# A linear attention with its forward decays moved into the projection, scores issued one tile early, backward keys on GpSimd, and norms taken tile by tile

## The reference, cut to what matters

```
la = log_sigmoid(l_a @ w2 + b) / 16            # per direction, 4 heads x 64
b = cumsum(la within a chunk of 64)             # the backward direction on flipped tokens
a = (q*exp(b - b_ref)) @ (k*exp(b_ref - b)).T, lower triangle
o = a @ v + (q*exp(b)) @ s_in
u = (k*exp(b_last - b)).T @ v;  s_next = exp(b_last)*s + u
y = rmsnorm_head(o_f)*g*silu(g_f) + rmsnorm_head(o_b)*g*silu(g_b)
```

## Time and profile before

| | |
|---|---|
| median of 3 runs | 1501.27 us (1497.28 to 1501.35) |
| the profiled execution | 1498.48 us, span 1496.7 us |
| busy, share of the span | PE 88%, PEld 68%, DVE 55%, ACT 46%, POOL 7% |
| chain that ended last | PE 75%, DVE 10%, DMA 7%, ACT 5% |
| mean granted TensorE clock | 0.948 of 2.4 GHz |
| projection of layer 0 ends | 213.15 us (216.72 less the wait of 3.57) |
| attention's first scores, layer 0 | 286.15 us |
| projection of layer 1 ends | 873.81 us |
| attention's first scores, layer 1 | 952.07 us |

### The profile page before, as it was taken

The page is one execution under the profiler, slowest core; times in us unless marked ns, Lnnn a source line. Parts: engine busy times, 40 slices in busy tenths (PEclk is TensorE's granted clock), DMA queues, the critical chain, the costliest instruction groups (busy, mean ns, idle before and its releaser), DMA issues.

```text
span 1496.7 us, 19449 instructions
## 1 busy us (share of the span) xinstructions
PE 1313.9 (88%) x7024; PEld 1020.9 (68%) x7024; DVE 817.0 (55%) x1174; ACT 691.3 (46%) x989; POOL 104.8 (7%) x93
## 2 busy tenths in 40 slices
PE   4799977679899999999989957795899999999993
PEld 0576655357688888888869843484688888888882
DVE  0412277773533332323343484654688988898882
ACT  2622343263532311322243452354577877787771
POOL 4000010001111100111210010020000000000001
PEclk9899998799999999999989979898899999999997
DMA  9365623201122321223212428343799999999992
GB/s 347 116 231 202 231 74 140 86 1 56 58 99 88 127 83 68 99 99 123 88 46 99 157 104 312 115 167 135 267 349 389 369 356 360 384 369 358 357 351 99
DMA packets 96383, 282.76 MB, mean 189 GB/s; under 512 B 8577, under 2 KB 10017, under 8 KB 96193
## 3 DMA queue, kind: packets, MB, share of 16 engines
q1 hardware_dynamic: 90592, 262.17, 48.1%
q0 software_dynamic: 3568, 12.19, 2.2%
q10 hardware_dynamic: 2160, 7.55, 1.4%
HBM read 271.39 MB, written 10.49 MB: 188 GB/s over the span
## 4 chain that ended last, share of the span: by engine, by line
PE 75%; DVE 10%; DMA 7%; ACT 5%; issue 3%; POOL 0%; POOLq 0%; ACTq 0%; SPq 0%; DVEq 0%
PE ps L635 12%; PE ps L636 12%; PE ps L637 12%; PE ps L1008 5%; PE ps L1010 5%; PE ps L1009 5%; DMA raw<-in_w_mod 3%; PE ps L612 3%; PE ps L1022 3%; PE ps L1024 3%; PE ps L1026 3%; DVE wlo L529 2%; DMA raw<-in_w_fm 1%; PE ps L870 1%; PE ps L707 1%
## 5 line engine op out<-in xcount | busy, mean ns | idle before, releaser
L529 DVE TENSOR_TENSOR wlo<-raw,whi 128x1024 fp32r<-128x1024 f32 (+2 forms) x271 | 349.1, 1302 | 310.8 <-ACT whi L524 309.9
L524 ACT ACTIVATE whi<-raw 128x1024 fp32r<-128x1024 f32 (+2 forms) x271 | 298.7, 1108 | 297.4 <-PE ps L637 147.9
L635 PE MATMUL ps<-hhi,whi 128*128 128x512 f32 (+1 forms) x736 | 277.6, 377 | 23.7 <-DVE hlo L1569 22.6
L636 PE MATMUL ps<-hlo,whi 128*128 128x512 f32 (+1 forms) x736 | 273.9, 372 | 0.0
L637 PE MATMUL ps<-hhi,wlo 128*128 128x512 f32 (+1 forms) x736 | 273.7, 372 | 0.0
L635 PEld LDWEIGHTS ps<-hhi,whi 128*128 128x128 f32 x736 | 139.6, 190 | 60.5 <-issue 29.6
L636 PEld LDWEIGHTS ps<-hlo,whi 128*128 128x128 f32 x736 | 139.9, 190 | 26.5
L637 PEld LDWEIGHTS ps<-hhi,wlo 128*128 128x128 f32 x736 | 139.4, 189 | 27.1
L529 DVE TENSOR_TENSOR xlo<-raw,xhi 128x1024 fp32r<-128x1024 f32 (+1 forms) x98 | 131.9, 1353 | 19.4 <-ACT xhi L524 17.2
L524 ACT ACTIVATE xhi<-raw 128x1024 fp32r<-128x1024 f32 (+1 forms) x98 | 113.3, 1165 | 44.4 <-PE ps L1026 33.3
L1008 PE MATMUL ps<-whi,hs_hi 128*128 128x512 f32 (+1 forms) x256 | 96.3, 376 | 2.5 <-DVE hs_lo L1895 2.5
(11 more groups left out here) (279 smaller groups left out, 2076.3 us busy)
## 6 DMA issues: line engine op xcount, KB each, us to landing
raw<-in_w_gu SPq DMA_DIRECT2D x230, 512.0 KB, 5.4
raw<-in_w_dn SPq DMA_DIRECT2D x80, 704.0 KB, 8.7
raw<-in_w_mod SPq DMA_DIRECT2D x96, 512.0 KB, 4.7
raw<-in_w_fm SPq DMA_DIRECT2D x32, 512.0 KB, 3.5
raw<-in_w_out SPq DMA_DIRECT2D x16, 512.0 KB, 4.8
raw<-in_w_tg SPq DMA_DIRECT2D x8, 512.0 KB, 3.5
y_rows<-back POOLq DMA_DIRECT2D x1, 4096.0 KB, 16.8
y_rows<-ys ACTq DMA_DIRECT2D x8, 512.0 KB, 4.6
```

The costliest lines, as they stand in the source:

```text
L524: nc.scalar.activation(high(v)[:, 0:cols], src[:, 0:cols], ACT.Copy).then_inc(hi_ready, 1)
L529: nc.vector.tensor_tensor(low(v)[:, 0:cols], landed_in(v)[0][:, 0:cols], high(v)[:, 0:cols].bitcast(F32), ALU.subtract).then_inc(lo_ready, 1)
L635: nc.tensor.matmul(outp, whs, xh, start=first, stop=False)
L636: nc.tensor.matmul(outp, whs, xl, start=False, stop=False)
```

## The change

- The forward logits are multiplied after SB. ACT takes their absolute value and softplus behind the split issued at SB+1, with a table load before and, after SC+1, one back; DVE does minimum, sum and scan there (`decay_sum`, `decay_scan`), the keys at SC and the reference keys at SC+1. The first gate unit on PE waits for the forward scan (`d_ready` of 1), as it writes the same banks.
- In `gla` PE issues tile m+1's scores ahead of tile m's outputs, the modulation pairs behind the outputs, and turns the backward keys at step 3 ahead of that step's outputs. ACT's and DVE's orders follow that. The backward minimum moves behind state 0, the backward scan to step 1.
- GpSimd multiplies the backward keys and reference keys (`later_keys`), behind its six memsets.
- Squares and norms are taken for all forward outputs at once (group 0) and for each backward tile apart (`squares`, `normed_heads`, `head_norms`); PE turns each tile when it is ready.

```diff
+                def logits(l, dr):
+                    for p in range(GT):
+                        nc.tensor.matmul(ps[:, 2 + 2 * dr + p, :], w2[32 * dr:32 * dr + 32, l, p * P:(p + 1) * P],
+                                         la[32 * dr:32 * dr + 32, :], start=True, stop=True).then_inc(z_done[l], 1)
...
+                        if m == SB:
+                            pe.wait_ge(v_out[l], NTT)
+                            logits(l, 0)
                         if m == AQ:
 
                             pe.wait_ge(g_out[l], len(list(gla_reads(l))))
-                            for dr in range(2):
...
+                            logits(l, 1)
...
                         if m == 0:
-                            pe.wait_ge(v_out[l], NTT)
+                            pe.wait_ge(d_ready[l], 1)
                         tm(v, m, 512, 2 if l else 0)
...
+                for n, (dr, step, t) in enumerate(todo):
+                    m = rd.index(n) if n in rd else None
+                    if m is not None and issued[0] == m and n == 0:
+                        pe.wait_ge(kt_out[l], GT)
+                        scores(m)
+                    updates(n)
+                    if n == NTT - 1:
+                        keys_turned(1)
+                    if m is not None:
+                        if issued[0] == m:
+                            scores(m)
+                        if m + 1 < len(rd) and todo[rd[m + 1]][0] == dr:
+                            scores(m + 1)
+                        outputs(m)
+                    if n == 0:
+                        pe.wait_ge(z_out, l + 1)
+                    if n == NTT - 1:
+                        pe.wait_ge(kt_out[l], 2 * GT)
+                    for k in gla_pairs(l, n):
+                        mod_pair(PAIR_GLA[l] + k)
...
-                    if kind == "fm" and f == AQ + 1:
+                    if kind == "fm" and f == SB + 1:
                         logits_abs(l, 0)
+                        nc.scalar.preload_act_table_set("natural_log_exp_and_others")
                         softplus(l, 0)
-                    if kind == "fm" and f == AQ + 2:
+                    if kind == "fm" and f == SC:
                         key_exp(l, 0)
-                    if kind == "fm" and f == AQ + 3:
+                    if kind == "fm" and f == SC + 1:
                         ref_exps(l, 0)
+                        nc.scalar.preload_act_table_set("silu_and_others")
...
+            def later_keys(l):
+
+                pool.wait_ge(zeroed[l], 3)
+                pool.wait_ge(e_ready[l], 5)
+                nc.gpsimd.tensor_tensor(gk[:, :, :], gk[:, :, :], lk[:, :, :], ALU.mult).then_inc(e_used[l], 1)
+                pool.wait_ge(at_done[l], len(gla_reads(l)))
+                pool.wait_ge(e_used[l], 5)
+                pool.wait_ge(e_ready[l], 7)
+                nc.gpsimd.tensor_tensor(gkp[:, :, :], gt2[1], lk[:, :, :], ALU.mult).then_inc(e_used[l], 1)
...
-                    if kind == "fm" and f == AQ + 1:
+                    if kind == "fm" and f == SB + 1:
                         logits_min(l, 0)
-                        log_decay(l, 0)
-                    if kind == "fm" and f == AQ + 2:
+                        decay_sum(l, 0)
+                        decay_scan(l, 0)
+                    if kind == "fm" and f == SC:
                         decayed_keys(l, 0)
-                    if kind == "fm" and f == AQ + 3:
+                    if kind == "fm" and f == SC + 1:
                         ref_keys(l, 0)
...
+                projected(dve, l)
+                queries(l, 0, gqp)
+                rope(l, AT - 1)
+                rope(l, AT)
+                dve.wait_ge(e_ready[l], 4)
+                queries(l, 0, gqb)
+                for n, (dr, step, t) in enumerate(todo):
+                    if n == NTT:
+                        dve.wait_ge(e_used[l], 6)
+                        dve.wait_ge(at_done[l], len(reads))
+                        queries(l, 1, gqp)
+                        dve.wait_ge(e_ready[l], 8)
                         dve.wait_ge(o_done[l], len(reads))
-                    queries(l, dr, gqp)
...
+                        queries(l, 1, gqb)
+                    if n in rd:
+                        masked(rd.index(n))
+                    states(n)
+                    if n == 0:
                         logits_min(l, 1)
...
+                    for k in gla_pairs(l, n):
+                        mod_step(PAIR_GLA[l] + k)
+                    if n == 0:
+                        decay_sum(l, 1)
+                    if n == 1:
+                        decay_scan(l, 1)
+                    if n == 2:
+                        ref_decay(l, 1)
+                    if n >= NTT:
+                        for g in [[], [], [0], norms_at(l, 2)][step]:
+                            normed_heads(l, g)
+                        for g in norms_at(l, step):
+                            squares(l, g)
+                last = len(last_tiles(l))
+                squares(l, last)
                 mods_in((PAIR_GLA[l] + GLA_PAIRS[l]) // 2)
...
+                for g in range(last - 1, last + 1):
+                    normed_heads(l, g)
```

More of the change, by code:

```diff
@@ new lines, in updates @@
+                        pe.wait_ge(rope_ready[l], AT + 1)
+                    if n == 1:
+                        pe.wait_ge(z_out, l + 1)
+                    if n >= 2:
+                        pe.wait_ge(st_ready[l], 2 * (n - 1))
+                    for c in range(2):
+                        for h in range(4):
+                            p, hh = h // 2, h % 2
+                            mm = nc.tensor.matmul(
+                                ps[CH * hh:CH * hh + CH, (6, 4)[n % 2], (2 * c + p) * CH:(2 * c + p + 1) * CH],
+                                gkt[:, t, c, h * CH:(h + 1) * CH], vt[:, t, P + h * CH:P + (h + 1) * CH],
+                                start=True, stop=True)
@@ new lines, in updates, with scores @@
+                    mm.then_inc(u_done[l], 1)
+                def scores(m):
+                    dr, step, t = todo[rd[m]]
+                    pe.wait_ge(e_used[l], 4 * dr + 3)
+                    if m == 0:
+                        pe.wait_ge(zeroed[l], 1)
+                    if m >= 2:
+                        pe.wait_ge(am_ready[l], m - 1)
+                    for p in range(GT):
+                        mm = nc.tensor.matmul(ps[:, m % 2, 2 * p * P:2 * (p + 1) * P],
+                                              gkp[:, p, t * P:(t + 1) * P], gqp[:, :, p, t * P:(t + 1) * P],
+                                              start=True, stop=True)
+                    mm.then_inc(at_done[l], 1)
+                    issued[0] = m + 1
@@ new lines, in outputs @@
+                def outputs(m):
+                    dr, step, t = todo[rd[m]]
+                    pe.wait_ge(am_ready[l], m + 1)
+                    pe.wait_ge(e_used[l], 4 * dr + 4)
+                    if m == 0:
+                        pe.wait_ge(zeroed[l], 3)
+                    pe.wait_ge(st_ready[l], 8 * dr + 2 * step + 1)
+                    if m >= 2:
+                        pe.wait_ge(o_out[l], m - 1)
+                    bank = 2 + m % 2
+                    for h in range(4):
+                        pv0 = P + h // 2 * P
+                        nc.tensor.matmul(ps[:, bank, h * P:(h + 1) * P], am[:, dr, h * P:(h + 1) * P],
+                                         vt[:, t, pv0:pv0 + P], start=(h == 0), stop=False,
+                                         skip_group_check=True)
+                    for ci, c in enumerate(gla_chunks(dr)):
+                        for h in range(4):
+                            p, hh = h // 2, h % 2
+                            o0 = h * P + hh * CH
+                            mm = nc.tensor.matmul(
+                                ps[CH * c:CH * c + CH, bank, o0:o0 + CH],
+                                gqb[:, hh, p, t * P + CH * c:t * P + CH * c + CH],
+                                state[:, dr, 2 * step + ci, p * CH:(p + 1) * CH],
+                                start=False, stop=(ci == 1), skip_group_check=True)
+                    mm.then_inc(o_done[l], 1)
@@ L1225, in gla, with keys_out @@
             def gla(l):
[L1226 to L1231 removed]
+                todo, rd = gla_steps(), read_steps(l)
+                def keys_out(dr):
                     for p in range(GT):
@@ new lines, in states @@
+                def states(n):
+                    dr, step, t = todo[n]
+                    if step == 0:
+                        dve.wait_ge(dec_ready[l], dr + 1)
+                    dve.wait_ge(u_done[l], n + 1)
+                    for ci, c in enumerate(gla_chunks(dr)):
+                        for p in range(GT):
+                            col = p * NCH + 2 * t + c
+                            ins = V.scalar_tensor_tensor(
+                                state[:, dr, 2 * step + ci + 1, p * CH:(p + 1) * CH],
```

(6 more changed lines are left out.)

301 lines of the change are left out of this document (127 added, 174 removed).

## The result

The changed kernel took 1514.16 us (median of 4 runs, 1512.76 to 1516.43), the kernel before 1500.58 in the same comparison (4 runs, 1497.28 to 1501.35): ratio 1.0097, 95% interval 1.0080 to 1.0115. It is slower by about 14 us. The two profiled executions lie 17.9 apart (spans 1514.6 and 1496.7), more than 14, since that of the changed kernel was the slowest of its four (1516.43) and that of the kernel before lay under its median (1498.48).

What follows compares the result with a forecast made beforehand. A serial DVE, ACT and PE chain was taken to bound layer 0's linear attention, PE the projection. 8.3 - 2.0 + 7.25 - 4.1 = +9.4 us on 1498.48 gave 1507.9, 1510 against the median; the forecast's own range was 1503 to 1518.

Steps and rivals of the forecast that it cites:

- The stall: Before each layer's first gate unit, PE waits for DVE's forward scan: 6.5 us in layer 0, 5.5 in layer 1.
- The clock: After each projection wait, part of the gate unit runs at half clock: +1.8 us in each layer.
- Two logits matmuls moved ahead take 1.0 us, so the later place gives 1.0 back: In the projection, two of four logits matmuls (2.0 us together) move ahead, adding 1.0 there and saving 1.0 later.
- The fourth gate unit about 1 us late: In layer 1's projection, ACT's added work makes the fourth unit's split about 1 us late, partly hidden by the slow clock.
- Layer 0's linear attention 2.0 shorter: Stretch from layer 0's last projection matmul to the first attention scores, 73.0 before, becomes 2.0 us shorter.
- The lead: In layer 0's linear attention the first outputs come 5.7 us sooner, then most of that is given back.
- E: End of PE's last projection matmul, from which linear attention is counted; before the change 213.15 in layer 0, 873.81 in layer 1.
- the replay: Linear attention worked through step by step with the old durations; layer 0's step 7 outputs at + 60.65, 0.4 us ahead.
- The turn behind the outputs: In odd linear-attention steps DVE waits some 2.5 us for turned modulation rows, as PE issues the outputs first.
- GpSimd's products 3.4 each: In the linear attention GpSimd's two 1024-column products take 3.4 us each, both covered; + 2.6 if each took 5.
- rival 3: DVE and GpSimd hold each other up in layer 0's linear attention; DVE loses 1.3 us, total 1509.2; chance 0.12.
- The backward minimum also has left this chain: In layer 0's linear attention, DVE's backward minimum no longer stands in the chain to the first outputs, 5.7 us ahead.

Runs made afterwards that it cites:

- e3_ahead: Changed kernel with ACT's and DVE's forward decay work put ahead of the splits of its step, in layer 0 alone: 1510.65 us, 1.0080 of the kernel before.
- e2_pair: e1_min with two further products, results unread, behind the forward logits at SB; one execution: in layer 0 both pairs stand between 121.03 and 123.0.
- e1_turns: Changed kernel with the modulation row's turn issued ahead of a step's outputs, not behind them: 1507.13 us, 1.0048 of the kernel before.
- e4_minimum: Changed kernel with forward decays at LQ (layer 0: ahead of splits), turn ahead of outputs, layer 1's backward absolute values, minimum and scan put back: 1486.54 us.
- e1_min: Changed kernel with PE's first gate unit waiting for DVE's forward minimum alone, not the scan difference: 1506.92 us, 1.0056 of the kernel before.

## Why the prediction was right in its sign and short in its size

- **The stall**: right. 6.46 and 5.71 us against 6.5 and 5.5, released by the scan difference, and in layer 0 through the chain told (ACT behind a split that waits for weights). Both ends of layer 0's stall came 2.0 us later than forecast (PE ready at 149.49, the difference done at 155.89), so its length held. e3_ahead shows that cause for layer 0: the first gate unit's wait goes when ACT's work stands ahead of the split.
- **The clock**: right. Half clock (the level of 1.2 GHz) follows both stalls. PE's products come 0.43 apart and not 0.23 for some 4.7 us in layer 0 and 3.7 in layer 1, which is 2.1 and 1.7 us lost against 1.8 and 1.8.
- **"Two logits matmuls moved ahead take 1.0 us, so the later place gives 1.0 back"**: this step failed. It divided 2.0 us by two. The two directions run side by side, so each place takes 1.98 and nothing comes back: +2.0 a layer instead of 0, 4.0 in all (e2_pair). Of layer 0's +12.4, 1.2 stood there already before the logits (123.23 against 122.08, where PE went on before).
- **The fourth gate unit about 1 us late**: not seen.
- **Layer 0's linear attention 2.0 shorter**: +0.4. The lead was right as far as step 2: outputs at E + 13.6, + 18.1 and + 26.0 against + 13.4, + 18.2 and + 26.2. Those of step 7 came at + 63.7, not + 60.65. By the trace these 3.1 us are mostly the clock, which the replay held at full rate: after idles of 2.75, 2.89 and 2.74 us the outputs of steps 2, 4 and 6 took 2.4, 3.1 and 3.3 us and not 1.9, and the pair behind the first of them 1.89 and not 1.04. The delay enters where DVE waits for PE: the state update of step 3 stands 1.11 us for PE's update behind that pair, and the outputs of step 3 are 1.2 us late. No run takes the clock alone away. The end took 9.8 us from there, near the 10.3 of the replay.
- **The turn behind the outputs**: right, and on the chain: moving it ahead gave 5.4 us in layer 0 (e1_turns).
- **GpSimd's products 3.4 each**: 2.35. The hold of rival 3 is real, but it falls on DVE alone: its difference took 3.13 us and not 1.22, while GpSimd, which had begun 0.3 us earlier, took the same 2.35 as without an overlap. The Trainium skill says (SBUF — State Buffer, Who interferes with whom) that one of the two is blocked. The trace agrees in layer 0; in layer 1 no DVE instruction with both inputs in SBUF overlapped them. The 1.3 us of rival 3 did not come about, since the second product was done 2.35 us before its reader, and the held difference didn't delay the state update of step 3, which waited for PE.
- **"The backward minimum also has left this chain"**: true in layer 0. For layer 1 the prediction left the minimum out as well, and there the step failed. That the stretch came out near the forecast (74.7 against 74.2, the first pairs at E + 14.7 against + 14.6) is luck. The forecast granted a lead of 4.2 us, but the forward keys were turned 7.6 us sooner (E + 4.9, + 12.5 before), and the minimum's new place took 3.8 of that back (PE held for 4.06 us, 0.23 before). Pairs at E + 9.6 are to be had, and with the minimum, its absolute values and the scan in their old places the stretch was 8 us shorter (e4_minimum).

The sum missed by 4 us on the medians (1510 against 1514; 1507.9 and 2.8 make 1510.7) and by 8.5 on the profiled executions (+9.4 against +17.9). The second place of the products (4.0), what is put down to the clock in the linear attention (3.1) and the 1.2 that stood in layer 0 before the change's first instruction are nearly all of the latter. The last is within the scatter of traces: with the same program up to there, the logits stood at 119.06 in e1_min and at 123.42 in e3_ahead.

## What to carry to other kernels

Work slipped in between weight splits must be put by what the engine waits for there: behind a split that waits for DMA it started late in both units tried, and ahead of it, it delays whatever else shares the place. When a reader of a PSUM bank is moved, look up every writer of that bank and what is queued behind the writer: here a minimum moved behind a state update held an update, four pairs and a scan. A time of several matmuls may not be divided by their number; see first whether they run side by side.

## What the runs showed of the hardware

- Matmuls with 32 contracted rows on rows 0 to 31 and on rows 32 to 63 of the array overlap fully: two directions' products in 1.98 us, as one's. On the same rows, the second pair came after the first.
- In that serial run of 32-row products in layer 1 the granted clock fell from 0.98 (837 to 838) to 0.50 (838 to 839), while PE's rows show no idle; the next tile's products of 256 columns followed 0.21 us apart and not 0.12. That was one execution.
- In the linear attention of layer 0 the granted clock was 0.50 soon after idles of 2.7 to 2.9 us (the first: 1.00 at 251 to 252, 0.72 at 252 to 254, 0.50 at 254 to 256), and stayed at full clock after one of 0.8 (at 289.26).
- GpSimd multiplied two 128x1024 operands in 2.35 us, where its 512-column sum took 1.72. A DVE difference of the same size (1.22 alone) that began behind it took 3.13, and GpSimd's time stayed 2.35.
